# The order of six matmuls in a chunk of a dense product: left half of the tokens first, then the right half

## What is computed

```python
def trunk_layer(x, ...):                       # x: 544 tokens x 2048
    z = rmsnorm(x, norm_mix_g) @ w_in          # 2048 x 6176 (with the gates)
    y_a = gated_conv(z); y_b = nsa_mixer(z); y_c = gdn_mixer(z)
    mix = concat(rmsnorm(y_a), rmsnorm(y_b), y_c)
    h = x + mix @ w_out                        # 2048 x 2048
    up = causal_dwconv(rmsnorm(h) @ ffn_up)    # 2048 x 11264
    ga, gv = split(up)
    return h + (silu(ga) * gv) @ ffn_down      # 5632 x 2048
```

## Time and profile before

| | |
|---|---|
| Median of 3 runs | 3084.39 us |
| Lowest and highest | 3083.86 and 3089.42 us |
| Profiled execution, its own time | 3087.0 us |
| Its span from first to last instruction | 3084.8 us |
| TensorE busy (matmuls) | 2920.5 us, 95% |
| VectorE, ScalarE, GpSimdE busy | 1125.6, 829.7, 130.2 us |
| Mean granted TensorE clock | 0.956 |

### The profile page before, as it was taken

How to read it: one execution, slowest core, us unless ns; L and a number is a source line. 1 busy time by engine, 2 the same in 40 slices (tenths; PEclk the granted TensorE clock), 3 DMA queues, 4 the chain that set the end, 5 groups by cost and what they waited for, 6 DMA issues and landing times.

```text
span 3084.8 us, 53533 instructions
## 1 busy us (share of the span) xinstructions
PE 2920.5 (95%) x21887; PEld 2826.4 (92%) x21887; DVE 1125.6 (36%) x1635; ACT 829.7 (27%) x1453; POOL 130.2 (4%) x297
## 2 busy tenths in 40 slices
PE   6999999978899788699899999999999999999999
PEld 5999999968778666699799999999999999999999
DVE  3332224427310552422444433444334443244432
ACT  3222226630202342312422212222222222122221
POOL 0000000000000000000011100111001110011100
PEclk9999999989769786899899999999999999999999
DMA  5232222210241002233122233222232222322223
GB/s 189 88 100 86 88 88 82 79 61 1 74 154 57 26 1 82 70 110 109 50 86 88 76 90 99 89 88 78 85 97 88 88 82 85 99 89 88 84 79 130
DMA packets 91780, 261.03 MB, mean 85 GB/s; under 512 B 10274, under 2 KB 27202, under 8 KB 89458
## 3 DMA queue, kind: packets, MB, share of 16 engines
q1 hardware_dynamic: 88562, 245.77, 25.0%
q10 hardware_dynamic: 2992, 13.01, 1.3%
q0 software_dynamic: 144, 1.11, 0.1%
HBM read 247.54 MB, written 16.50 MB: 86 GB/s over the span
## 4 chain that ended last, share of the span: by engine, by line
PE 72%; DVE 3%; ACT 1%; issue 1%; DMA 0%; SPq 0%; DVEq 0%; ACTq 0%; PEldq 0%
PE ps L535 70%; PE ps L539 1%; DVE x_whole L1455 1%; DVE x_lo L1459 1%; DVE arena L1776 0%; DVE arena L1774 0%; ACT arena L1320 0%; DMA arena<-in_state_gdn 0%; SPq L460 0%; DVE arena L1632 0%; DVE arena L1712 0%; DMA arena<-in_ffn_w 0%; ACT x_hi L1092 0%; DVE arena L1624 0%; ACT L1056 0%
## 5 line engine op out<-in xcount | busy, mean ns | idle before, releaser
L535 PE MATMUL ps<-x_hi,w_hi 128*128 128x272 f32 x4896 | 1018.5, 289 | 41.0 <-DVE w_lo L1464 23.5
L1464 DVE TENSOR_TENSOR w_lo<-w_whole,w_hi 128x1024 fp32r<-128x1024 f32 (+2 forms) x432 | 486.4, 1126 | 1451.4 <-ACT w_hi L1101 1443.0
L535 PE MATMUL ps<-x_hi,w_lo 128*128 128x272 f32 x4896 | 1009.4, 288 | 0.0
L535 PE MATMUL ps<-x_lo,w_hi 128*128 128x272 f32 x4896 | 1008.4, 288 | 0.0
L1101 ACT ACTIVATE w_hi<-w_whole 128x1024 fp32r<-128x1024 f32 (+2 forms) x432 | 422.5, 979 | 1567.7 <-PE ps L535 1565.0
L535 PEld LDWEIGHTS ps<-x_hi,w_hi 128*128 128x128 f32 x4896 | 765.9, 189 | 48.1 <-DVE w_lo L1464 24.4
L535 PEld LDWEIGHTS ps<-x_lo,w_hi 128*128 128x128 f32 x4896 | 768.2, 189 | 0.0
L535 PEld LDWEIGHTS ps<-x_hi,w_lo 128*128 128x128 f32 x4896 | 765.4, 189 | 0.0
L535 PE MATMUL ps<-arena 128*128 128x128 f32 (+15 forms) x2684 | 508.9, 358 | 85.3 <-ACT arena L1082 24.7
L535 PEld LDWEIGHTS ps<-arena 128*128 128x128 f32 (+5 forms) x2684 | 420.8, 229 | 156.7 <-issue 40.9
L535 PE MATMUL ps<-act_lo,w_hi 128*128 128x272 f32 x1408 | 290.4, 287 | 0.0
(11 more groups left out here) (191 smaller groups left out, 1047.8 us busy)
## 6 DMA issues: line engine op xcount, KB each, us to landing
w_whole<-in_w_up SPq DMA_DIRECT2D x176, 512.0 KB, 3.4
w_whole<-in_w_proj SPq DMA_DIRECT2D x96, 512.0 KB, 3.7
w_whole<-in_w_dn SPq DMA_DIRECT2D x64, 384.0 KB, 3.1
w_whole<-in_w_dn SPq DMA_DIRECT2D x64, 320.0 KB, 2.9
w_whole<-in_w_o SPq DMA_DIRECT2D x32, 512.0 KB, 3.5
arena<-in_w1c SPq DMA_DIRECT2D x8, 1024.0 KB, 7.6
arena<-in_cache_kt SPq DMA_DIRECT2D x48, 128.0 KB, 3.6
arena<-in_x_t SPq DMA_DIRECT2D x4, 1088.0 KB, 16.3
```

The lines of the kernel that those rows point to most:

```text
L535: return e.matmul(out, lhsT, rhs, start=start, stop=stop, skip_group_check=True)
L1464: e.tensor_tensor(wlo[h % 2][:, 0:n], raw[h % SLOTS][:, 0:n], whi_f[h % 2][:, 0:n], ALU.subtract).then_inc(w_lo, 1)
```

## The change

In `unit`, the loop over the three products of a chunk issued each product for the left half and then for the right half. Now an outer loop goes over the halves, and the three products of the left half come first, then the three of the right half. Which matmuls there are, their operands, their banks, their start and stop flags and all semaphores stay as they were; the gates' own loop (L608 to L614) is not changed.

```diff
-                        for n, (w, x) in enumerate(((wh, xs[0]), (wh, xs[1]), (wl, xs[0]))):
-                            start, stop = c == 0 and n == 0, c == sum(tiles) - 1 and n == 2
-                            a, b = halves(x[:, c])
-                            mm(bank(banks, HN), w, a, start, stop)
-                            last = mm(bank(banks + 1, NT - HN), w, b, start, stop)
+                        for side in range(2):
+                            for n, (w, x) in enumerate(((wh, xs[0]), (wh, xs[1]), (wl, xs[0]))):
+                                start, stop = c == 0 and n == 0, c == sum(tiles) - 1 and n == 2
+                                last = mm(bank(banks + side, HN), w, halves(x[:, c])[side], start, stop)
```

## The result

| | before | after |
|---|---|---|
| Median of 5 runs | 3087.47 us | 3103.25 us |
| Lowest and highest | 3083.86 and 3090.04 | 3102.37 and 3104.22 |
| Span of the profiled execution | 3084.8 | 3101.1 |

The ratio is 1.0053, with a 95% interval from 1.0038 to 1.0068: the new order is slower by half a per cent, some 16 us, where no change was forecast. It lies just outside the stated range too. The kernel before has two more runs here than the three that the prediction worked from, which moves its median from 3084.39 to 3087.47 us.

What follows compares the result with a forecast made beforehand. The prediction took TensorE's unbroken matmul stream, products times start interval, to bound the kernel. Weights, banks and waits summed as 0 + 0 + 0, giving 3084 us, range 3069 to 3102, with chance 0.68 of no change.

Steps and rivals of the forecast that it cites:

- What bounds the kernel: Output projection and ConvFFN: unbroken matmul runs, time is products times start interval, 124.5 ns (normed tokens) and 125.0 ns (activations).
- Weights: Within each chunk: weights change at four of six handovers instead of two; taken as zero, bound 15 us saved.
- The 3 ns: Timeline steps between normed-token product pairs: those without a weight change averaged 251 ns, those with one 248 ns.
- PSUM banks: Four of six handovers per chunk now stay in their bank, 12,544 in all; taken as zero.
- both directions: Bank handovers: staying in a bank could cost up to 63 us, or fewer bank changes could save up to 78 us.
- Waits: Semaphores stay on the last matmul of a half and unit; left bank completes 0.37 us earlier, nobody is told; no gain.
- The sum: Whole kernel: 0 + 0 + 0 on the time before, so 3084 us.
- the fourth rival: Product stream: remainder depends on which load runs beside which product; 9 us either way, 3075 or 3093; chance 0.07 faster, 0.06 slower.
- Its sign: Start intervals of the two stages: one that moves in one stage alone would speak for the fourth rival.

Runs made afterwards that it cites:

- e1_swap: Against the kernel before: halves and banks still alternate, but product order changes the weights at four of six handovers; 3090.51 us (1.0012).
- e3_new_alt: Operands in the changed kernel's order, but the six products go to the two banks in turn; 3102.29 us, ratio to before 1.0045.
- e4_old_runs: Operands in the order of the kernel before, but a chunk's first three products go to one bank, last three to the other; 3086.41 us (0.9996).
- g1_off256: Kernel before, old order, but products for the right half read their 272 columns from column 256 instead of 272; 3117.38 us (1.0101).
- s1_w_old: Kernel before, but eight ConvFFN stretches read weight tiles 0 to 96 words earlier, except each half's first tile; 3095.98 us beside 3086.85 before.
- g3_all_left: Changed kernel's order and banks, but all six products of a chunk read the left half; 3112.12 us (1.0084).

## Why the prediction was wrong, step by step

**What bounds the kernel**: right. The time is products times interval; 14 of 16 us appear there, and no wait was added.

**Weights**: zero was right, as far as the normed tokens can show: e1_swap changes them as often as the changed kernel and keeps 1792.0 cycles. The 3 ns by which the steps with a change seemed shorter belong to positions, not to weights: the same six intervals appear when other products stand there.

**PSUM banks**: zero was right in both directions, shown by e3_new_alt and e4_old_runs, which give each order's cycles with the other's way of using the banks. The rows had bounded the two directions only at 63 and 78 us, so the zero between them was a choice.

**Waits**: right, as the rows after show.

**The sum** failed, because a term was missing: the places from which successive products read, and their sequence. The nearest thing that I had named is the fourth rival (which load runs beside which product), with a chance of 0.13 and a size of 0.5 ns a product, taken from the difference of the two stages; measured were 0.83 ns for the normed tokens and 0.44 ns for the activations. What I put against it, that the same loads and products stay in the chunk and that what belongs to each alone sums to the same, is the step that was wrong: the price does not belong to each alone. The rival was not right as I had put it either. Its sign, an interval that moves in one of the stages alone, did not come out, since both moved. And modulo 256 bytes the pairs of load and product are the same ones in the up stage, where all weight tiles are alike (512 bytes from tile to tile, 8192 from w_hi to w_lo): in either order three left and two right products run beside a load of their own chunk, and one right product beside the first load of the next. The sums are 1792 and 1804. So the price of a product isn't that of its pair: what ran before it enters as well, as the two sequences of g1_off256 also show.

What is shown, then: the distance of two starts is the columns plus a rest of some 27 cycles; the rest depends on the start of the moving operand modulo 256 bytes, on that of the weight tiles, and on the sequence; banks and changes of weights do not enter. That the two reads get in each other's way is the natural reading, since either address alone moves the result and a shift of 128 bytes in the weights exchanges even and odd chunks; it is argued, and no run shows the reads themselves. The Trainium skill, "TensorE: Matmul & The Clock Gate", section "Step-by-step: what each phase is for", says that weights and moving operand have a read port each and that a load takes no bandwidth from a running matmul. s1_w_old does not agree that a load leaves the stream alone: only the load's address changes there, and a chunk changes by up to 20 cycles in the mean (1793.3 to 1813.3). Here the measurement decides. How the chip arbitrates, and why the rest is 27 cycles and not less, stays open. None of the layouts and orders beat the kernel before by more than the 3 cycles of one stretch (1788.7), whose right half overlaps the left and so gives other sums; a layout with the same starts modulo 256 bytes and no overlap was not run.

## What to carry to other kernels

In this kernel's dense stream of matmuls, each with its own weight load, the start addresses of both operands are part of the schedule: moving the weights by 64 bytes or reordering reads of the same tiles each shifted a stage by up to 1%, and the effect of the order changed its sign with the layout. When a reorder that changes no count and no wait still changes the time, average the distance of successive starts by position before looking for a stall, and repeat the comparison in a second layout before calling one order better. An argument that the same operations sum to the same time needs their sequence to be irrelevant, and that has to be measured.

## What was not expected of the hardware

The intervals are exact: of the 1641 chunks without a stop in 103 units of the kernel before (output projection and up stages), 99.7% take 1784 or 1800 cycles to within one nanosecond, the step of the trace, and the means are 1784.0 and 1800.1. Two kernels that read different tokens in a different order of tiles, g1_off256 and g3_all_left, agree for the normed tokens by position to 0.1 cycle; the places that they read agree modulo 1024 bytes. One kernel with eight variants in its loops therefore measures differences of 0.1%, which timing whole runs of this kernel, with a scatter of 6 us in 3087, could not.
